# The first layer's queries: both row halves written from the bank by ScalarE and VectorE, in place of GpSimd's copies

## The reference

```python
qa, ka, va, ga, qs, ks, vs, gs = split_cols(x @ w_in, EVEN_SPLITS)
# group A, 4 heads, each with two maps m of width 64
s = jnp.einsum('bqhmd,bkhmd->bhmqk', qb, ka).astype(jnp.float32) * (A_DH ** -0.5)
s = s - slopes[None, :, None, None, None] * dist
p = jax.nn.softmax(jnp.where(visible, s, -jnp.inf), axis=-1)
w = p[:, :, 0] - lam * p[:, :, 1]
# group B, 8 heads of width 64, stick-breaking
z = jnp.einsum('bqhd,bkhd->bhqk', qb, ks).astype(jnp.float32) * (B_DH ** -0.5)
log_skip = jnp.where(earlier, jax.nn.log_sigmoid(-z), 0.0)
a = jnp.where(earlier, jnp.exp(jax.nn.log_sigmoid(z) + log_pass), 0.0)
```

## Time and profile before

| | before |
|---|---|
| runs, median (lowest to highest) | 1375.52 us (1375.06 to 1375.91) |
| profiled execution | 1375.03 us, span 1373.2 us, mean granted clock 0.993 |
| busy TensorE, VectorE, ScalarE, GpSimd | 1319.9, 876.7, 547.6, 488.4 us |
| first layer's attention stage | about 39 to 660 us |
| second layer's attention stage | about 940 to 1280 us |

### The profile page before, as it was taken

The page is one execution under the profiler, slowest core; times in us unless marked ns, Lnnn a source line. Parts: engine busy times, 40 slices in busy tenths (PEclk is TensorE's granted clock), DMA queues, the critical chain, the costliest instruction groups (busy, mean ns, idle before and its releaser), DMA issues.

```text
span 1373.2 us, 22469 instructions
## 1 busy us (share of the span) xinstructions
PE 1319.9 (96%) x8400; PEld 1242.5 (90%) x8400; DVE 876.7 (64%) x1973; ACT 547.6 (40%) x1290; POOL 488.4 (36%) x465
## 2 busy tenths in 40 slices
PE   8999999999899999997999999998999999999997
PEld 8999999999799999996888999998998989989886
DVE  5776869595587847668465323554767667677465
ACT  3443546463545535355111011533445445446200
POOL 3323232223234232347333323563433234335431
PEclk9999999999999999998999999999999999999999
DMA  6000111001011011113133211222111112106141
GB/s 221 32 32 31 47 32 47 16 31 47 32 39 40 22 42 51 59 41 123 58 122 133 94 46 38 86 81 70 40 47 39 47 36 71 57 20 199 61 163 76
DMA packets 47355, 88.26 MB, mean 64 GB/s; under 512 B 4480, under 2 KB 30080, under 8 KB 47120
## 3 DMA queue, kind: packets, MB, share of 16 engines
q1 hardware_dynamic: 44800, 78.45, 17.4%
q10 hardware_dynamic: 2448, 8.39, 1.6%
HBM read 66.84 MB, written 19.98 MB: 63 GB/s over the span
## 4 chain that ended last, share of the span: by engine, by line
PE 51%; DVE 4%; issue 2%; ACT 2%; POOL 2%; DVEq 0%; ACTq 0%; POOLq 0%
PE bank L1965 20%; PE bank L2109 13%; PE bank L2033 7%; PE bank L2083 5%; PE bank L2053 4%; DVE pb L1745 1%; ACT rtmp L1355 1%; PE bank L2004 1%; PE bank L2131 1%; POOL wsp L1046 1%; POOL pb L1235 0%; DVE ring L1760 0%; POOL big L1089 0%; DVE qpe L1621 0%; DVE qpe L1625 0%
## 5 line engine op out<-in xcount | busy, mean ns | idle before, releaser
L1965 PE MATMUL bank<-big,wsp 128*128 128x344 f32 (+2 forms) x3024 | 557.9, 328 | 6.4 <-DVE big L1562 3.3
L1965 PEld LDWEIGHTS bank<-big,wsp 128*128 128x128 f32 x3024 | 480.6, 189 | 10.2 <-POOL wsp L1046 4.7
L1045 POOL TENSOR_SCALAR wsp<-wraw 128x1024 fp32r<-128x1024 f32 (+3 forms) x92 | 83.6, 908 | 538.6 <-PE bank L1965 418.3
L1760 DVE TENSOR_TENSOR ring<-bank,ring 128x256 fp32r<-128x256 f32 (+3 forms) x292 | 156.5, 553 | 82.8 <-ACT ring L1437 79.9
L1437 ACT ACTIVATE ring<-bank 128x256 fp32r<-128x256 f32 (+3 forms) x292 | 138.7, 495 | 149.5 <-PE bank L2053 107.4
L2109 PE MATMUL bank<-big,wsp 128*128 128x512 f32 x816 | 195.9, 398 | 0.0
L1046 POOL TENSOR_TENSOR wsp<-wraw,wsp 128x1024 fp32r<-128x1024 f32 (+3 forms) x92 | 186.6, 2028 | 7.7
L2083 PE MATMUL bank<-ring,vtok 128*128 128x256 f32 (+2 forms) x1276 | 183.2, 281 | 2.3 <-DVE ot L1772 1.2
L2109 PEld LDWEIGHTS bank<-big,wsp 128*128 128x128 f32 x816 | 152.9, 189 | 34.8 <-DVE big L1799 0.4
L2083 PEld LDWEIGHTS bank<-ring,vtok 128*128 128x128 f32 (+1 forms) x1276 | 171.8, 191 | 7.9 <-issue 4.0
L1965 PE MATMUL bank<-h1t,wsp 128*128 128x344 f32 (+2 forms) x1080 | 173.8, 322 | 1.5 <-DVE lraw L1610 1.5
(11 more groups left out here) (133 smaller groups left out, 1435.7 us busy)
## 6 DMA issues: line engine op xcount, KB each, us to landing
wraw<-in_w SPq DMA_DIRECT2D x47, 512.0 KB, 3.5
wraw<-y_scratch SPq DMA_DIRECT2D x17, 448.0 KB, 3.7
woraw<-in_wo SPq DMA_DIRECT2D x12, 512.0 KB, 4.9
y_scratch<-ot SPq DMA_DIRECT2D x40, 128.0 KB, 1.7
xres<-in_x SPq DMA_DIRECT2D x8, 512.0 KB, 4.6
h_scratch<-res ACTq DMA_DIRECT2D x8, 512.0 KB, 2.7
gate_scratch<-gtmp SPq DMA_DIRECT2D x8, 512.0 KB, 2.9
gate<-gate_scratch SPq DMA_DIRECT2D x8, 512.0 KB, 3.6
```

The lines of the kernel that those rows point to most:

```text
L1045: pool.wait_ge(S["pool_step"], tick(nc.gpsimd.tensor_scalar(hi, raw, 1.0, 1.0, ALU.mult, ALU.mult)))
L1760: V.tensor_tensor(R[0:rows, r % NRING, 1, 0:w], bank[T_BANK[t]][0:rows, 0:w], lo_hi(R[0:rows, r % NRING, 0, 0:w]), ALU.subtract).then_inc( ...
L1965: ins = mm(dst, wsp[:, SLOT[kind, u], a, k, :], rhs[:, b, k0 + k, c0:c0 + w], start=(k == 0 and a == 0 and b == 0), stop=last)
```

## The change

ScalarE writes each map's high half twice, to rows 0 to 63 and 64 to 127, and VectorE the low half twice, both from the bank, with the low half always computed against the high half in rows 0 to 63. GpSimd's copies of `q0` are gone, and TensorE waits for VectorE's evacuation (`proj_evac`) in place of `q_copied`. The planned durations follow: a `q0` chunk is 1400 ns of ScalarE and 1800 of VectorE in place of 700, 870 and 1400 of GpSimd. The second layer's `qr` is as it was.

```diff
@@ weave
-            copied = ("P", "qr", u - u % 2, cq) if layer else ("P", "q0", u, cq)
-            after += [("pool", copied)] if copied in within else []
-            after += [evacuated(("P", "qn", u, cq))] if layer else []
+            copied = ("P", "qr", u - u % 2, cq)
+            after += [("pool", copied)] if layer and copied in within else []
+            after += [evacuated(("P", "qn" if layer else "q0", u, cq))]
@@
-        a, d = {"k0": (700, 870), "q0": (700, 870), "g0": (360, 440), "g1": (360, 440), "rms0": (0, 580),
+        a, d = {"k0": (700, 870), "q0": (1400, 1800), "g0": (360, 440), "g1": (360, 440), "rms0": (0, 580),
@@
-            L.put("pool", "Q", s, 1400 if kind == "q0" else 900, [("dve", s)], 70)
+            if kind == "qr":
+                L.put("pool", "Q", s, 900, [("dve", s)], 70)
@@ copy_queries
-                    if kind == "q0":
-                        to, from_ = qst[64:128, m, :, cc], qst[0:64, m, :, cc]
-                    elif m == 0:
+                    if m == 0:
@@ gpsimd
-                if s[0] == "P" and s[1] in ("q0", "qr"):
+                if s[0] == "P" and s[1] == "qr":
                     copy_queries(s)
@@ evacuate, scalar
                     for m in range(2):
-                        ins = A(qst[0:64, m, 0, cc], src[64 * m:64 * m + 64, 0:w], ACT.Copy, scale=q_scale(u))
+                        for to in (0, 64):
+                            ins = A(qst[to:to + 64, m, 0, cc], src[64 * m:64 * m + 64, 0:w], ACT.Copy, scale=q_scale(u))
@@ evacuate, vector
                     for m in range(2):
-                        ins = V.scalar_tensor_tensor(
-                            out=qst[0:64, m, 1, cc], in0=src[64 * m:64 * m + 64, 0:w],
-                            scalar=q_scale(u), in1=lo_hi(qst[0:64, m, 0, cc]), op0=ALU.mult, op1=ALU.subtract)
+                        for to in (0, 64):
+                            ins = V.scalar_tensor_tensor(
+                                out=qst[to:to + 64, m, 1, cc], in0=src[64 * m:64 * m + 64, 0:w],
+                                scalar=q_scale(u), in1=lo_hi(qst[0:64, m, 0, cc]), op0=ALU.mult, op1=ALU.subtract)
@@ scores, tensor
+                    pe.wait_ge(S["proj_evac"], EVAC_AT["P", "qn" if layer else "q0", u, cq])
                     if layer:
-                        pe.wait_ge(S["proj_evac"], EVAC_AT["P", "qn", u, cq])
-                    pe.wait_ge(S["q_copied"], Q_COPY["P", "qr" if layer else "q0", u - u % 2 if layer else u, cq])
+                        pe.wait_ge(S["q_copied"], Q_COPY["P", "qr", u - u % 2, cq])
```

More of the change, by code:

```diff
@@ L634, in count_before @@
     return out
-Q_COPY = count_before(PROJ, lambda s: s[1] in ("q0", "qr"))
+Q_COPY = count_before(PROJ, lambda s: s[1] == "qr")
 ROTATED = count_before(PROJ, lambda s: s[1] in ("kpe", "qr"))
```

## The result

The changed kernel took 1378.5 us (median of 12 runs, 1374.9 to 1379.2) beside 1375.3 us for the kernel before. The ratio is 1.0017, with a 95% interval of 1.001 to 1.0025; eleven more runs on another chip gave 1.0019 (1.001 to 1.0027). The ratios are those of the means and give 2.3 and 2.6 us; by the medians here it is 3.3 us. So it is slower by about 2.5 us, by the ratio under the 0.2% that the prediction took as the limit of no change. It is not the 5.6 us faster that was forecast, and 1378.5 lies just above the range of 1365.0 to 1378.3. The profiled execution took 1375.8 us, of which 1374.0 span.

The account below looks back on a forecast made before the run. TensorE was taken as the bound (96% busy), with 17.3 us of gaps within reach. Terms -8.2 - 1.7 + 1.1 + 1.0 + 1.2 + 1.0 = -5.6 us gave 1370.0 us from 1375.5, range 1365.0 to 1378.3.

Parts of the forecast that it names:

- Removed: First layer's attention: TensorE's nine waits for GpSimd's copies go, -8.2 us, and -1.7 us of clock.
- First and third chunks: Query waits: eight first chunks 1.0 us more with 1.1 kept; third chunks of units 4 to 7 keep 1.2.
- the rival: Unit 5's third chunk: planner lets a scan go ahead of the queries, wait 1.1 us; rival's chance 0.22.
- Given back: VectorE's scans beside GpSimd: some 1.9 us lost at one place, part to the copies; no gain in the sum.
- the signs: Busy times if right: VectorE 22 to 25 us up, ScalarE 22 up, GpSimd 40 down.
- The prediction's 0.98 us for a scan "alone": VectorE's scan of 400 alone takes 0.98 us; two beside GpSimd's split and copies need 3.85.
- Moved, 1.0 us: Work behind the added writes: 2% of 24.5 us more VectorE work is 0.5; took 1.0, bound 9.1.
- the dip's 1.7: Behind the 2.63 us wait at 358.02: TensorE's lower clock for 3.4 us loses 1.7 us, regained without that gap.
- the 3.2 that the sum has for chunks and queue together: The sum's added costs: first chunks 1.0, third chunks 1.2, work behind the added writes 1.0 us.
- the rival that made VectorE's queue the bound: VectorE's 24.5 us more reach TensorE; at 45% they cost 11 us, kernel takes 1379.9; chance 0.16.
- The rival "the wait moves to VectorE": Waits at first and third chunks and the queue leave 1.1 us gained, 1374.4 us, no change; chance 0.22.
- A new order, 3 us either way: First layer's stage replanned: from zero, 3 us either way; about 1 us a unit, partly cancelling over eight.

Follow-up runs that it names:

- e1: The change's work (four writes on each engine, no copies) in the order of the kernel before (planner told 700, 870, 1400): 1384.7 us, ratio 1.0082.
- e8: All the change's writes, no copies, in the order of before, ScalarE filling rows 64 to 127 from SBUF beside VectorE: 1369.2 us, ratio 0.9955.
- e5: Order of before; VectorE writes low halves to both row halves, ScalarE writes once, GpSimd copies the high halves beside VectorE: 1373.9 us, ratio 0.9990.
- e4: Order of before; ScalarE writes high halves to both row halves, VectorE writes once, GpSimd copies the low halves only: 1378.3 us, ratio 1.0020.
- e2: The work of the kernel before (copies and single writes) in the order of the changed kernel (told 1400, 1800, 0): 1392.9 us, ratio 1.0131.
- e6: The change with ScalarE filling rows 64 to 127 from SBUF beside VectorE, in its own order (told 930 + 930 and 2090): 1381.7 us, ratio 1.0049.
- e9: VectorE writing low halves twice, GpSimd copying high halves beside it, in an order of its own (told 930, 2090, 1050): 1384.7 us, ratio 1.0066.

## Why the prediction was wrong

**Where the change puts its cost.** With one TensorE list, stretches from unit 0's meta scores to unit 4's (group A), and from there to the end of the first output blocks (group B; 687.35 us in before), compare one to one. Columns as in the earlier trace rows; before, then e1 (all writes), then e8 (all writes, early handover):

```profile
38.99:340.22 301.23, 295.83 (x1958) 284.01 (x1958) 221.78 (x685) 144.05 (x316) 83.53 (x62) 1.00 0.11 36
340.22:687.35 347.13, 329.86 (x2138) 309.31 (x2139) 232.73 (x372) 155.76 (x375) 131.01 (x100) 0.98 0.16 50
```

```profile
39.65:351.48 311.83, 300.26 (x1958) 287.16 (x1959) 228.67 (x709) 155.22 (x340) 64.89 (x38) 0.99 0.10 35
351.48:696.63 345.15, 326.36 (x2139) 306.27 (x2139) 237.69 (x394) 165.27 (x397) 110.51 (x78) 1.00 0.16 50
```

```profile
40.97:342.57 301.60, 295.65 (x1960) 284.20 (x1959) 228.65 (x709) 154.78 (x340) 65.02 (x38) 1.00 0.11 36
342.57:682.87 340.30, 328.00 (x2141) 308.15 (x2139) 236.92 (x394) 164.92 (x397) 110.49 (x78) 0.98 0.16 51
```

| against before | VectorE behind the bank at a chunk (wait for ScalarE's writes + its own) | queries ready after | group A | group B |
|---|---|---|---|---|
| e5, VectorE twice | 0.9 + 2.1 us | 3.2 us | +0.2 | -1.4 |
| e4, ScalarE twice | 1.9 + 1.1 | 4.15 | +2.8 | -1.8 |
| e8, both, early | 0.9 + 2.1 | 3.1 | +0.4 | -6.8 |
| e1, both, late | 1.9 + 2.1 | 4.1 | +10.6 | -2.0 |

e1 and e8 have the same busy VectorE (228.7 and 228.7 us in the first stretch) and ScalarE (155.2, 154.8) and differ by 10.2 us there. So it isn't the load of the two engines; it is the handover. TensorE's waits in e1's first stretch show where it is felt:

```profile
PE bank L2053 <- DVE pb L1736: 4.2, 5, 1.3
PE bank L2033 <- DVE qst L1591: 2.5, 7, 0.5
PE bank L2033 <- DVE stat L1692: 2.3, 5, 1.3
```

In before these are 2.5 us for the weights, 0.7 for the copies in the queries' place, and 0.6 for the maxima. So 1.8 us come at the queries themselves and 3.4 behind them, at the weights and maxima. Before to e1, TensorE's gaps grow by 6.2 us and its busy time by 4.4. Of the latter, 3.4 us come from two stretches of 3.4 us each at the lower clock, half of full speed, that before lacks (from 126 and from 204.6 us).

The reading that fits is that VectorE's queue stands for four writes of ScalarE and then holds for four of its own, with a group's maxima and weights behind. It is argued from these rows. No run parts the stand of the queue from the later queries, since e8 shortens both by 1 us; e4 has e1's stand and queries as late as e1's, but VectorE's own two writes less, and loses 2.8 us where e1 loses 10.6. So, as far as these runs go, it takes both, the wait and the longer hold.

**Point by point.** *Removed:* right. The copies' 8.2 us are gone from the list, and near 358 us the clock has no dip in either trace of the changed kernel; it has others, as behind 228 us. *First and third chunks:* near. Eight first chunks wait 3.0 us in sum (2.1 forecast), a second chunk 0.45, third chunks of units 4 to 7 1.2 (1.2 forecast). The last is luck in part: it isn't 0.3 for each but 0.2, 1.0 and twice nothing, and the 1.0 is unit 5's, where three scans go ahead of the queries, as the rival said (1.1). *Given back:* 7 us of VectorE's time, where the signs had 22 to 25 us more and it was 17.6. The added writes are unstretched, 516 ns in the mean against 513 before. The Trainium skill, SBUF — State Buffer, section "Who interferes with whom", says that a VectorE instruction with at most one SBUF input, outside the modes that use two ports for one tensor, doesn't contend with GpSimd. The trace agrees, with these 516 ns. The prediction's 0.98 us for a scan "alone" was in fact beside GpSimd's split at 439.11 us; one with GpSimd idle, at 349.18, takes 0.99, so its number holds.

*Moved, 1.0 us:* this step failed. I took a rate from the whole stage, 9.1 us of gaps to 416.7 us of VectorE's work, and multiplied it with the added busy time. On the same order the runs show +10.1 us, with the copies' 8.2 us and the dip's 1.7 gone, so some 20 us of cost (3.4 of them at new stretches of lower clock) in place of the 3.2 that the sum has for chunks and queue together. A mean rate says nothing of a late step ahead of a chain, and the wait for ScalarE, which isn't busy time, was named in the text but left out of the product. What was measured is near the rival that made VectorE's queue the bound, though that one was priced by busy time too, which e5 and e8 refute.

*The gain of group B* was 7.1 us of waits plus the clock. e1 got 2.0 of it, e8 6.8. Even the 2.0 are no gain in waits: TensorE's busy time fell by 3.5 us there, with a clock of 1.00 for 0.98, and its gaps grew by 1.5 (in e8 they fell by 5.0). In e1 the waits moved on to the low halves of the turned weights, L1760, which VectorE now makes later. TensorE's list in the second stretch, before:

```profile
PE bank L2033 <- POOL qst L1147: 7.6, 6, 2.6
PE bank L2053 <- DVE ring L1760: 6.8, 6, 3.1
...
PE bank L2083 <- DVE ring L1760: 0.7, 1, 0.7
```

and e1:

```profile
PE bank L2053 <- DVE ring L1760: 8.9, 7, 3.1
PE bank L2083 <- DVE ring L1760: 4.7, 3, 1.7
```

That is 6.1 us more where 7.6 went. In e8 the two rows are 6.3 and 2.1 us, 0.9 more than before. The rival "the wait moves to VectorE" named the mechanism, but looked for it at the queries.

*A new order, 3 us either way:* mis-sized. Orders for the same work lay 11.7 us apart with the late handover (1373.0 and 1384.7), 12.5 with the early one (1369.2 and 1381.7), and 7.4 with the copies (1367.9 and 1375.3), or 25 with e2. A bad place comes three times, in units 1 to 3, as with 3 x 2.6 us here; so differences didn't cancel over the units as I assumed. The order of the change was worth 6 to 8 us to its work (1384.7 to 1378.5 or 1377.1) and still had 7.7 us of new gaps. So the small net error hides two large ones: a cost 17 us over the forecast, and an order 6 to 8 us better where nothing was forecast.

**Is the change itself good or bad?** The early handover beats the late one in both fixed orders (15.5 and 8 us); that is shown. In the one order made for it, it didn't (1381.7 against 1373.0 to 1378.5 for the late one in its own). Whether writing the queries without GpSimd beats the copies is not: -6 us in one order, +8 in the other. What stays open is a rule for which order suits which work; none of the plans here was good at telling it, and the lowest time found, 1367.9 us, comes from the kernel before with other numbers for its planner.

## What to carry to other kernels

On a kernel like this one, price an added instruction by how long its engine's queue stands, its wait for another engine included, and by which chain is behind it, not by its busy time and not with a mean rate. When two engines write the same thing in turns, hand over after the half that the second needs, and let the first finish from a place that doesn't hold the second up; here that was worth 15.5 and 8 us in two fixed orders. Where the order comes from a planner, swap work and order (the new work in the old order, and the old in the new) to see which of them a difference belongs to, and try several orders for each way of doing the work before comparing the two. Measured durations are worth trying but are no guarantee: they gave 7 us to the kernel before and 4 to the change, and took 12 us from the early handover (e6 against e8) and 11 from e5's work (e9).

## What was not expected of the hardware

Identical gaps of 2.58 us were followed by TensorE's lower clock level (1.2 GHz) in one execution and not in the next (0.66 and 1.00 over the same 5 us), so one profile can't tell how many such stretches a kernel has. A fall can also stand behind short gaps: in the trace of e1, these of 0.53, 0.18 and 0.86 us are the largest ahead of the one at 204.6 us:

```profile
195.47 0.89 PE L2033 MATMUL bank<-kst,qst 128*128 128x16 f32 x6 [0.53 <-DVE qst L1591]
200.62 0.64 PE L2033 MATMUL bank<-kst,qst 128*128 128x400 f32 x2 [0.18 <-DVE qst L1591]
202.12 0.18 PE L2053 MATMUL bank<-eye,pb 16*16 16x16 f32 x1 [0.86 <-DVE pb L1736]
```

The clock is 0.79 from 204 to 205 us and 0.50 from 205 to 208. Ten projection products that took 1.87 us in before (from 196.13) take 2.91 there (from 204.10). Nearly the same three gaps stand in unit 1 (117.77 to 124.44 us), with a fall at 126, and in unit 3 (272.46 to 279.12 us), with none.
